# A decoder trunk on one core: the buffer of the down and output projections' activations is moved from the end of SBUF to its beginning

## The reference

```
h = h + stick_breaking_mixer(rmsnorm(h), w_qkv, w_o)       # layer 0
h = h + (silu(n @ w_gate) * (n @ w_up)) @ w_down           # n = rmsnorm(h), D_FF = 5632
h = h + chunked_gmlp_mixer(rmsnorm(h), w_in, ..., w_o)     # layer 1
h = h + (silu(n @ w_gate) * (n @ w_up)) @ w_down
out = rmsnorm(h)
```

## The kernel before, in words

| buffer | bytes | before | after | before, mod 64 |
|---|---|---|---|---|
| h | 16,384 | 16,512 | 106,624 | 0 |
| xT | 32,768 | 32,896 | 123,008 | 0 |
| raw | 16,384 | 65,664 | 155,776 | 0 |
| w_hi | 16,384 | 82,048 | 172,160 | 0 |
| w_lo | 16,384 | 98,432 | 188,544 | 0 |
| gate | 4,096 | 114,816 | 204,928 | 0 |
| res | 4,096 | 118,912 | 209,024 | 0 |
| rstd_row, gain_bc | 9,216 | 123,008 | 213,120 | 0 |
| ident | 512 | 132,224 | 222,336 | 0 |
| region | 90,112 | 139,232 | 16,512 | 32 |

## Time and profile before

### The profile page before, as it was taken

The page is one execution under the profiler, slowest core; times in us unless marked ns, Lnnn a source line. Parts: engine busy times, 40 slices in busy tenths (PEclk is TensorE's granted clock), DMA queues, the critical chain, the costliest instruction groups (busy, mean ns, idle before and its releaser), DMA issues.

```text
span 2171.5 us, 30354 instructions
## 1 busy us (share of the span) xinstructions
PE 2157.2 (99%) x10993; PEld 1826.3 (84%) x10993; DVE 1210.9 (56%) x1216; ACT 1062.4 (49%) x1212; POOL 15.9 (1%) x29
## 2 busy tenths in 40 slices
PE   9999999999999999999999999999999999999998
PEld 7888887888888888888888888888888888888886
DVE  5556565555656565544444565555656565554443
ACT  5555554555545455444345444555555454544433
POOL 1000000000000000000000000000000000000000
PEclk9999999999999999999999999999999999999999
DMA  7555545566565656555556565556665656555553
GB/s 254 183 167 165 180 147 172 176 193 191 181 198 175 202 174 202 190 182 181 193 184 202 178 207 171 181 182 186 190 188 184 196 178 201 177 201 185 186 188 139
DMA packets 207127, 402.43 MB, mean 185 GB/s; under 512 B 12304, under 2 KB 12896, under 8 KB 206688
## 3 DMA queue, kind: packets, MB, share of 16 engines
q1 hardware_dynamic: 206352, 398.51, 58.0%
q0 software_dynamic: 688, 3.18, 0.5%
q10 hardware_dynamic: 32, 0.01, 0.0%
HBM read 399.55 MB, written 2.10 MB: 185 GB/s over the span
## 4 chain that ended last, share of the span: by engine, by line
PE 99%; DMA 0%; issue 0%; DVE 0%; ACT 0%; SPq 0%; POOLq 0%; POOL 0%; DVEq 0%; ACTq 0%
PE acc L1019 17%; PE acc L1021 17%; PE acc L1020 17%; PE acc L1188 15%; PE tp L1188 15%; PE tp L1190 8%; PE acc L1190 8%; PE tp L1029 1%; PE tp L1278 0%; DMA h<-in_x 0%; PE tp L1085 0%; PE tp L1075 0%; PE tp L1099 0%; PE tp L1076 0%; PE tp L1098 0%
## 5 line engine op out<-in xcount | busy, mean ns | idle before, releaser
L633 DVE TENSOR_TENSOR w_lo<-raw,w_hi 128x1024 fp32r<-128x1024 f32 x751 | 909.3, 1223 | 712.2 <-ACT w_hi L340 712.0
L340 ACT ACTIVATE w_hi<-raw 128x1024 fp32r<-128x1024 f32 x751 | 790.6, 1060 | 807.4 <-PE acc L1021 447.2
L1188 PE MATMUL acc<-xT,w_hi 128*128 128x512 f32 x1408 | 519.8, 391 | 0.0
L1188 PE MATMUL tp<-xT,w_hi 128*128 128x512 f32 x1408 | 519.5, 391 | 0.0
L1190 PE MATMUL tp<-xT,w_lo 128*128 128x256 f32 x1408 | 394.2, 280 | 0.0
L1190 PE MATMUL acc<-xT,w_lo 128*128 128x256 f32 x1408 | 394.1, 280 | 0.0
L1019 PE MATMUL acc<-w_hi,hid_hi 128*128 128x512 f32 x944 | 375.3, 398 | 0.9 <-DVE hid_lo L708 0.9
L1021 PE MATMUL acc<-w_hi,hid_lo 128*128 128x512 f32 x944 | 374.2, 396 | 0.0
L1020 PE MATMUL acc<-w_lo,hid_hi 128*128 128x512 f32 x944 | 374.1, 396 | 0.0
L1188 PEld LDWEIGHTS tp<-xT,w_hi 128*128 128x128 f32 x1408 | 263.3, 187 | 57.9
L1188 PEld LDWEIGHTS acc<-xT,w_hi 128*128 128x128 f32 x1408 | 263.3, 187 | 57.7
(11 more groups left out here) (144 smaller groups left out, 856.8 us busy)
## 6 DMA issues: line engine op xcount, KB each, us to landing
raw<-in_ffn_w_gate_up SPq DMA_DIRECT2D x352, 512.0 KB, 4.3
raw<-in_ffn_w_down SPq DMA_DIRECT2D x176, 512.0 KB, 3.7
raw<-in_sb_w_qkv SPq DMA_DIRECT2D x95, 512.0 KB, 4.4
raw<-in_gm_w_in SPq DMA_DIRECT2D x64, 512.0 KB, 4.2
raw<-in_sb_w_o SPq DMA_DIRECT2D x32, 512.0 KB, 4.1
raw<-in_gm_w_o SPq DMA_DIRECT2D x32, 512.0 KB, 4.1
h<-in_x SPq DMA_DIRECT2D x3, 512.0 KB, 9.5
gain_bc<-in_gm_v_norm POOLq DMA_DIRECT2D x1, 1024.0 KB, 8.0
```

The lines of the kernel that those rows point to most:

```text
L340: nc.scalar.activation(w_hi[:, p % RING], raw[:, p % RING], ACT.Copy).then_inc(hi_ready, 1)
L633: nc.vector.tensor_tensor(w_lo[:, p % RING], raw[:, p % RING], w_hi[:, p % RING].bitcast(f32), ALU.subtract).then_inc(lo_ready, 1)
L1188: nc.tensor.matmul(dst, w_hi[:, p % RING, k, ns], xT[:, kt].rearrange("p v t -> p (v t)"), start=(kt == 0), stop=False)
```

## The change

The buffer that holds the region is allocated before all others instead of behind them. Nothing else differs: the same instructions, in the same order, with the same waits; only addresses change.

```diff
+        region = sb("region", [P, 2 * KF * S])
         h = sb("h", [P, RT, D])
         xT = sb("xT", [P, KD, 2, S], f32r)
         xT_hi, xT_lo = xT[:, :, 0], xT[:, :, 1]
...
         moments = sb("moments", [P, RT, 2])
 
 
-        region = sb("region", [P, 2 * KF * S])
         R0 = nc.lookup_mloc(region).addr
         HB = KF * S * 4
```

## The result

The changed kernel takes 2160.24 us (median of 5, 2160.19 to 2161.06) against 2171.9 us: 11.7 us or 0.54% less, ratio 0.9946 with an interval of [0.9935, 0.9957]. The forecast was 2150.0 us. The wide range, 2147 to 2173, held the time; the narrow one of the likeliest case, 2147 to 2153, did not. The gain is little more than half of what that case said, and in size the result is what the prediction called D, to which it gave 0.05. Its profiled execution took 2161.06 us with a span of 2159.3 us, 12.2 us less than the span before.

A forecast was written before the change was run, and what follows sets the result against it. The prediction took PE's own pace to bound the kernel. 21.9 us off for the region's held operands, and 0 for its small operands, moved buffers and lost cover, took 2171.9 to 2150.0 us; range 2147 to 2173.

The forecast's parts named there:

- likeliest case: Rival A's case, on which the predicted time rests: 2150.0 us, own range 2147 to 2153, chance 0.62.
- D: Gain on the region's matmuls holds, but late transfers or colliding streams give part back; 2152 to 2165 us, chance 0.05.
- The bound: Whole kernel: PE is busy 99% of the span, and nothing but its own pace sets the time.
- The first term: Matmuls holding hid_hi or hid_lo reach xT's pace: 2,880 x 7.6 ns, 21.9 us off.
- Rival A: The held operand's start within 64 bytes, or any larger power of two, sets the pace; 2150.0 us, chance 0.62.
- Rival C: Height in SBUF sets the pace, so gate and up and xT slow down; about 2203 us, chance 0.14.
- Rival B: The region's place does not matter and its matmuls keep their pace; 2171.9 us, chance 0.19.
- third, all that moves up by 22 x 4,096 bytes: Buffers moved up by the region's new place keep their remainders, so their move was to cost nothing: 0 us.

The follow-up runs named there:

- run 4: Kernel before the change, region still behind the large buffers but moved ahead of rows_first, to 135,296; xT and weights unmoved; 2159.97 us.
- run 1: Kernel before the change, with stats and moments moved behind the region, so that it starts at 139,008; 2167.01 us, in two groups 9 us apart.
- run 2: Kernel before the change, with only moments moved behind the region, so that it starts at 139,200; 2169.31 us.
- run 9: Changed kernel with small buffers moved around the region, putting it at 16,768 and 256 bytes apart from the weights; 2160.2 us.
- run 5: Changed kernel with total and rstd ahead of the region, at 16,640, while xT and weights keep remainders of 128; ratio 1.0004, in two groups.
- run 3: Changed kernel with minus_half ahead of the region, at 16,544, and total and moments behind it; 2169.59 us.
- run 10: Against run 6, total and rstd put ahead of xT, which starts 128 bytes apart from the weights; 2173.11 us.
- run 7: The changed kernel again without any edit; 2159.77 to 2160.31 us in four runs, ratio 0.9945.
- run 8: Changed kernel with one small matmul of line 1210 issued once more, only in the second layer; median 2152.48 us, in two groups 18 us apart.
- first four experiments: run 1, run 2, run 3 and run 4, which moved the region to other places; 2167.01, 2169.31, 2169.59 and 2159.97 us.
- run 6: Changed kernel with xT placed behind the weights instead of ahead of them, remainders by 4,096 kept; 2160.12 us.
- run 11: Changed kernel with the first small matmul of line 1210 issued twice more in both layers; 2160.64 to 2162.88 us in four runs.

## Why the prediction was right, and where it was half wrong

**The bound** was read rightly. PE's pace is all that sets the time, in every run. Nothing that waits, transfers or runs on ACT or DVE played a part, and rival D's mechanisms did not occur: no transfer came late, and the loss that gives the total D's size is there in run 4 too, where `xT` and the weights keep their old places.

**The first term** came out nearly to size. Taken from the starts in the two traces, the four stretches on `hid` got shorter by 2.4 us (the attention's output projection), 7.9, 2.8 (the gMLP's) and 8.0 us, 21.0 in all, where the sum had 21.9. The 7.6 ns hold in full where nothing interrupts, as in the last down projection (234.3 to 226.7 ns); in the attention's output projection only 6.2 ns a matmul were won. The chain bears it out: from the first line 1210 to the next transposes it takes 537.24 us instead of 539.39, 2.15 us less for 288 matmuls on `hid` (288 x 7.6 = 2.2).

**Its reason was wrong as put.** I took the start of the region within 64 bytes, since `xT`, `w_hi` and `w_lo` had one remainder there. They had one remainder by 4,096 too, and I could not tell these apart; runs 1 and 2 refute 64 and 128. Rival A named the larger powers of two as well, but as remainders of the operand by itself. What counts is the distance between the held and the streamed operand, by 256:

| run | region | w_hi | distance by 256 | ns on hid |
|---|---|---|---|---|
| changed kernel | 16,512 | 172,160 | 0 | 226.8 |
| 4 | 135,296 | 82,048 | 0 | 226.8 |
| 9 | 16,768 | 172,672 | 0 (256 by 512) | 226.7 |
| 1 | 139,008 | 82,048 | 128 | 232.3 |
| 5 | 16,640 | 176,256 | 128 | 232.4 |
| 2 | 139,200 | 82,048 | 64 | 233.4 |
| 3 | 16,544 | 172,288 | 160 | 233.4 |
| before | 139,232 | 82,048 | 96 | 234.3 |

It is the distance and not the remainder of the region alone: in run 3 `xT` and the weights both start at multiples of 256, and `xT` keeps 389 ns; in run 5 the region starts at one and is slow, because the weights don't. Run 10 shows that it holds for `xT` too, and in either role. That the change worked is luck in this respect: coming first happened to give the region the remainder of its partners, and with one small buffer ahead of it, as in run 3, it would have won 2.3 us.

Another partner would fit the table as well: `raw` has the remainder of `w_hi` in every run, and DVE, ACT and the transfers use it while PE works. The trace before settles this. In the last 6 us of its last down projection all pieces are prepared, and the others are idle, but the pace stays slow. The window (columns as above), and two starts of PE in it:

```profile
2154.00:2160.00 6.00, 6.00 (x28) 4.81 (x27) 0.05 (x1) 0.00 (x0) 0.00 (x0) 1.00 0.00 0
```

```profile
2154.13 0.40 PE L1019 MATMUL acc<-w_hi,hid_hi 128*128 128x512 f32 x1
...
2159.75 0.40 PE L1317 MATMUL acc<-w_hi,hid_hi 128*128 128x512 f32 x1
```

There are 24 matmuls from one start to the other, 5.62 / 24 = 234.2 ns each, with no transfer, nothing on ACT or POOL and 0.05 us on DVE. The loss lies between PE's own two operands.

**Rival C, height,** is refuted by run 4, and already by the first gate and up after the change, which keeps 346.8 ns a pair with `w_hi` at 172,160. Rival B, that the place doesn't matter, is refuted by the result.

**The step that failed** is "third, all that moves up by 22 x 4,096 bytes. The remainders stay, so by the reason that I follow it costs nothing". It stands as to addresses; what it missed is that the pace of gate and up is not fixed by addresses alone. The prediction took 346.8 ns a pair as a property of the operands. At these distances it is one of two rhythms, and 2,720 matmuls in a row keep the one that they fall into: 9.1 us lost whenever it is the slow one. That is shown by run 7 (same program, other stage slow) and by the profile of run 8 (both fast after an addition of 0.2 us); that both are slow in run 8's upper group follows from its totals alone. Adding it up: 21.9 - 9.1 = 12.8 us, or 21.0 - 9.1 = 11.9 with the measured first term, against 12.2 in the spans and 11.7 in the medians. So the time fell within the range because that was wide enough for B and D, not because anything in the prediction allowed for a second rhythm.

**What stays open.** The cause of the second rhythm is not shown. The kernel before never falls into it (31 runs beside the first four experiments lie within 2171.3 and 2173.0), and neither do runs 2 and 3; at distance 128 (runs 1 and 5) it takes one stage or none. At distance 0 all 25 runs without the single addition of run 8 and with the old order (the result, runs 4, 6, 7, 9 and 11) have the total of exactly one slow stage, which two independent draws would not give. So the second stage's rhythm depends on the first's. How it does is only argued: at distance 0 the matmuls of the last down projection start 226 or 227 ns apart throughout, and such a fixed rhythm could carry a phase from the one stage to the other; at distance 96 the spacing goes round between 231 and 238 ns. What the phase is measured against, I can't tell from these traces. Distances other than 0, 64, 96, 128 and 160 were not tried.

The Trainium skill, SBUF — State Buffer, Specifications (TRN2), puts a price on crossings of 16-byte lines, and all eight places in the table start on such a line, with paces from 226.7 to 234.3 ns; by that rule alone they would be equal, and the measurement decides against that. The same page of the Trainium skill, under Who interferes with whom, has PE's weight loads and streams on two independent read ports; that the distance between just these two operands matters, 226.7 against 234.3 ns, is at odds with it here.

## What to carry to other kernels

Where PE is busy throughout, compare the distance between matmul starts for the same line on different operands; 7 ns of 227 cost 1% of this kernel and show in no wait. Lay out held and streamed operands so that their starts leave the same remainder by 256 bytes, and check it again after any small buffer is added, since buffers in a row pass every odd size on. A long uninterrupted sequence can lock into a slower rhythm in some runs and not in others, or in one of two equal stages, so look at groups of times, not at a median, before an edit is credited or blamed for 9 us.

## What the runs showed of the hardware

- Held float32r operand 128 x 128, streamed 512 columns, clock at 2.4 GHz: 226.7 to 226.8 ns between starts at a distance of 0 by 256, 232.3 to 234.3 ns at 64, 96, 128 or 160. The slow pace stays (234.2 ns at 96) while the transfers and the other engines are idle. Transposes (128 columns) don't show it: 272 ns of record for `res` and for `k_s`, and 108.9 ns between starts for both.
- Gate and up's sequence of 512 and 256 columns runs at 346.7 or at 353.3 ns a pair at the same addresses, and keeps its rhythm for 2,720 matmuls; with `xT` and the weights 128 bytes apart by 256 it runs at 351.1. The steps of these paces are alike: 226.7 to 233.4 and 346.7 to 353.4 are both 6.7 ns.
- Totals come in groups 9 us apart (runs 1 and 5) or 18 us apart (run 8), with nothing between, while a group there is at most 1.8 us wide.
